# Moving chunk totals through memory in a hybrid trunk kernel, and reordering two small steps

## What is computed

```python
log_a = log_sigmoid(ab @ w_alpha + b_alpha) / B_GATE_TAU          # (S, 256), TAU = 16
g = cumsum(log_a over the 64 tokens of a chunk)
g_end = g[last token of the chunk]                                # the chunk's total
k_dec = k * exp(g_end - g)                                        # decay from token to chunk end
dS = k_dec^T v                                                    # per chunk and head
S_c = exp(g_end) * S_{c-1} + dS                                   # 8 chunks
o_t = q_t S_c
```

## Time and profile before

| | |
|---|---|
| median of 3 runs | 926.05 us (925.83 to 926.31) |
| the profiled execution | 926.16 us |
| its span, first to last instruction | 924.4 us |
| TensorE busy | 916.8 us |
| DVE busy | 609.8 us |
| ACT busy | 390.1 us |
| mean granted TensorE clock | 0.999 |

### The profile page before, as it was taken

One profiled execution on the slowest core, in us unless ns is written; L12 is line 12 of the kernel. 1 busy time (PEld: TensorE's weight loads), 2 busy tenths in 40 slices (PEclk: granted clock), 3 DMA queues, 4 the chain that ended last, 5 costly groups with the idle time before them and its releaser, 6 DMA issues.

```text
span 924.4 us, 13093 instructions
## 1 busy us (share of the span) xinstructions
PE 916.8 (99%) x5092; PEld 752.6 (81%) x5092; DVE 609.8 (66%) x1006; ACT 390.1 (42%) x728; POOL 31.7 (3%) x68
## 2 busy tenths in 40 slices
PE   9999999999999999999999999999999999999997
PEld 7988888888888777888889888888888887778886
DVE  7976468448567877575459655674567668876834
ACT  7453335224543454432444433442363425553324
POOL 0000000000000001000000000000000000100000
PEclk9999999999999999999999999999999999999999
DMA  8424325232534345422233423253235333444542
GB/s 294 126 93 137 114 69 159 91 102 83 154 113 134 90 137 161 137 90 92 92 115 94 125 92 112 62 169 96 88 114 160 103 115 115 133 143 137 150 124 91
DMA packets 42909, 110.98 MB, mean 120 GB/s; under 512 B 8608, under 2 KB 11552, under 8 KB 42720
## 3 DMA queue, kind: packets, MB, share of 16 engines
q1 hardware_dynamic: 36736, 100.62, 34.2%
q10 hardware_dynamic: 4064, 5.33, 2.1%
q0 software_dynamic: 2048, 4.20, 1.6%
HBM read 85.41 MB, written 2.23 MB: 95 GB/s over the span
## 4 chain that ended last, share of the span: by engine, by line
PE 94%; DVE 2%; ACT 2%; DMA 1%; SPq 1%; issue 0%; DVEq 0%; ACTq 0%
PE ring L671 72%; PE nat L671 9%; PE nat L879 3%; PE aux L902 2%; PE nat L858 1%; PE nat L686 1%; PE nat L685 1%; PE nat L687 1%; DMA raw<-pieces 1%; PE ring L686 1%; PE ring L685 1%; PE ring L687 1%; PE nat L749 1%; DVE merged L1227 1%; DVE w_lo L1249 1%; ACT work L1146 1%
## 5 line engine op out<-in xcount | busy, mean ns | idle before, releaser
L671 PE MATMUL ring<-act_hi,w_hi 128*128 128x512 f32 x784 | 307.9, 393 | 0.0
L671 PE MATMUL ring<-act_lo,w_hi 128*128 128x512 f32 x784 | 305.4, 390 | 0.0
L671 PE MATMUL ring<-act_hi,w_lo 128*128 128x512 f32 x784 | 305.1, 389 | 0.0
L919 ACT ACTIVATE w_hi<-raw 128x1024 fp32r<-128x1024 f32 x152 | 161.7, 1064 | 334.2 <-PE ring L671 260.5
L1249 DVE TENSOR_TENSOR w_lo<-raw,w_hi 128x1024 fp32r<-128x1024 f32 x152 | 184.6, 1216 | 97.8 <-ACT w_hi L919 97.6
L671 PEld LDWEIGHTS ring<-act_hi,w_hi 128*128 128x128 f32 x784 | 147.1, 188 | 38.0 <-issue 8.1
L671 PEld LDWEIGHTS ring<-act_hi,w_lo 128*128 128x128 f32 x784 | 147.2, 188 | 31.0
L671 PEld LDWEIGHTS ring<-act_lo,w_hi 128*128 128x128 f32 x784 | 147.2, 188 | 29.7
L1600 DVE SCALAR_TENSOR_TENSOR gates<-ring,rstd 128x512 f32<-128x512 f32 x72 | 49.3, 685 | 78.4 <-PE ring L671 78.3
L671 PE MATMUL ring<-y_hi,w_hi 128*128 128x512 f32 x192 | 74.9, 390 | 0.0
L671 PE MATMUL ring<-y_hi,w_lo 128*128 128x512 f32 x192 | 74.7, 389 | 0.0
(11 more groups left out here) (237 smaller groups left out, 1037.7 us busy)
## 6 DMA issues: line engine op xcount, KB each, us to landing
raw<-pieces SPq DMA_DIRECT2D x152, 512.0 KB, 3.5
bank_g<-work SPq DMA_DIRECT2D x80, 64.0 KB, 2.7
lat<-work SPq DMA_DIRECT2D x48, 64.0 KB, 2.8
bank_g<-work POOLq DMA_DIRECT2D x40, 64.0 KB, 2.5
bank_g<-work ACTq DMA_DIRECT2D x40, 64.0 KB, 3.2
xt<-x_t SPq DMA_DIRECT2D x8, 256.0 KB, 5.2
bank_a<-work SPq DMA_DIRECT2D x32, 64.0 KB, 2.0
bank_g<-bank_a SPq DMA_DIRECT2D x16, 128.0 KB, 3.9
```

The lines of the kernel that those rows point to most:

```text
L671: mm = pe.matmul(dst, stationary, moving, start=start and i == 0, stop=stop and i == 2)
L919: nc.scalar.activation(w_hi[:, n % HL, :], raw[:, n % RAW, :], ACT.Copy).then_inc(hi_split.sem, 1)
```

## The change

1. The chunk totals. The last column of each chunk in `later`, which was zero, now holds 1/TAU for the whole chunk, so the product of `gla_decay` has the chunk's total in the row of its last token. ACT takes Exp twice: once for all rows into `ends` (which lies where `soft` was), once with a per-partition factor `keep` (0 for the last token of a chunk, else 1) into `dec`. In `gla_end` 0, ACT saves the two total rows of each token tile to memory; in `gla_end` 1 it waits for these two saves, and issues two loads that read them back with channels on the partitions, straight into `decay`. The TensorE work of L812 and L815, the copy and the small Exps are gone, and `gla_end` no longer uses the `aux` bank. `gla_state` waits for the loads.
2. The tanh of the last gate piece of branch A moves from before `PUKV` to behind it. `y_lo` 3 stays where it was.
3. In branch C, `gate_c` 0 moves ahead of `divide_c` 2, and `y_hi`, `y_lo` of that output each move by one place.

```diff
@@ make_schedule
-        (63, ("y_hi", 3)),
-        (64, ("y_lo", 3))))
+        (63, ("y_hi", 3))))
     last_gate = todo.pop()
     piece(PUKV)
-    todo.append(last_gate)
+    step(last_gate, ("y_lo", 3))
...
-        (24, ("divide_c", 2)),
-        (25, ("gate_c", 0), ("turn_c", 2)),
-        (26, ("y_hi", TT)),
-        (27, ("y_lo", TT), ("send", 4)),
+        (24, ("gate_c", 0), ("divide_c", 2)),
+        (25, ("y_hi", TT), ("turn_c", 2)),
+        (26, ("y_lo", TT)),
+        (27, ("send", 4)),
...
-AUX = [s for s in SCHEDULE if s[0] in ("rms", "rstd_nat", "gla_end", "latent")]
+AUX = [s for s in SCHEDULE if s[0] in ("rms", "rstd_nat", "latent")]
@@ TensorE
-                    elif name == "gla_end":
-
-                        aux_bank(layer, u)
-                        if i == 0:
-                            for t in range(TT):
-                                mm = pe.matmul(aux[32 * t:32 * t + 32, 0:256], member, log_a[:, t, :], start=True, stop=True)
-                        else:
-                            for j in range(2):
-                                mm = pe.transpose(aux[:, j * P:(j + 1) * P], totals[:, j * P:(j + 1) * P], ident)
@@ ACT
-                        nc.scalar.activation(dec, nat_gate, ACT.Exp).then_inc(dec_set.sem, 1)
+                        nc.scalar.activation(ends, nat_gate, ACT.Exp).then_inc(ends_set.sem, 1)
+                        nc.scalar.activation(dec, nat_gate, ACT.Exp, scale=keep).then_inc(dec_set.sem, 1)
                     elif name == "gla_end":
-                        act.wait_ge(aux_ready.sem, aux_ready.at(layer, u + 1))
                         if i == 0:
-                            nc.scalar.activation(totals, aux[:, 0:256], ACT.Copy).then_inc(aux_free.sem, 1)
+                            act.wait_ge(ends_set.sem, ends_set.at(layer, 1))
+                            for c in range(2):
+                                act.dma_start(ends_dram[:, c:c + 1, :].rearrange("t c n -> c t n"), ends[CHUNK * c + CHUNK - 1:CHUNK * c + CHUNK, :, :]).then_inc(ends_saved.sem, 16)
                         else:
+                            act.wait_ge(ends_saved.sem, ends_saved.at(layer, 32))
                             for j in range(2):
-                                one = nc.scalar.activation(decay[:, NC * j:NC * j + NC].rearrange("p (t c) -> p t c", t=TT),
-                                                           aux[:, j * P:(j + 1) * P].rearrange("p (t m) -> p t m", t=TT)[:, :, 0:2],
-                                                           ACT.Exp)
-                            one.then_inc(aux_free.sem, 1)
+                                act.dma_start(decay[:, NC * j:NC * j + NC],
+                                              ends_dram[:, :, j * P:(j + 1) * P].rearrange("t c p -> p (t c)"), allow_slow_non_contiguous=True).then_inc(ends_placed.sem, 16)
@@ DVE
-                        dve.wait_ge(aux_free.sem, aux_free.at(layer, AUX.index(("gla_end", 1)) + 1))
+                        dve.wait_ge(ends_placed.sem, ends_placed.at(layer, 32))
@@ constants
+    for c in range(2):
+        out[t // CHUNK == c, LATER + CHUNK * c + CHUNK - 1] = 1 / B_TAU
-    out[:, MEMBER:MEMBER + 2] = (t[:, None] // CHUNK == np.arange(2)[None, :]) / B_TAU
+    out[:, KEEP] = t % CHUNK != CHUNK - 1
```

More of the change, by code:

```diff
@@ L289 @@
 PARAMS = 20
-IDENT, MEMBER = 0, 128
+IDENT, KEEP = 0, 128
 K_TABLE = 130
@@ L306, in at, with build_hybrid_trunk @@
         return layer * self.per_layer + (self.before + max(n, 1 - self.before))
-def build_hybrid_trunk(nc, x_t, pieces, params, alpha, tables, consts, final_g, out, k_rope_dram):
+def build_hybrid_trunk(nc, x_t, pieces, params, alpha, tables, consts, final_g, out, k_rope_dram, ends_dram):
     with ExitStack() as ctx:
@@ L352, in build_hybrid_trunk @@
         alpha_raw = bank_a[:, 2048 + P:2048 + P + DEPTH * 256].rearrange("p (l n) -> p l n", l=DEPTH)
-        later, member = bank_a[:, 2048:2048 + P], con[:, MEMBER:MEMBER + 32]
+        later, keep = bank_a[:, 2048:2048 + P], con[:, KEEP:KEEP + 1]
         prob = [*(work[:, i, :] for i in range(3)), bank_a[:, 3072:3584]]
@@ L381, in build_hybrid_trunk @@
         warm = merged[:, 7, :]
-        totals = work[:, 6, 0:256]
         o_nat = prob
@@ L395, in build_hybrid_trunk @@
         soft = gates[:, 8:10, :].rearrange("p a (t n) -> p (a t) n", t=2)
+        ends = soft
         log_a = gates[:, 10:12, :].rearrange("p a (t n) -> p (a t) n", t=2)
@@ L456, in build_hybrid_trunk @@
         gate_in, gate_log, decay_in, dec_set = sig("gate_in", 1), sig("gate_log", 1), sig("decay_in", 1), sig("dec_set", 1)
+        ends_set, ends_saved, ends_placed = sig("ends_set", 1), sig("ends_saved", 32), sig("ends_placed", 32)
         k_dec_set, v_a_set, v_b_set = sig("k_dec_set", TT), sig("v_a_set", TT), sig("v_b_set", TT)
@@ L1827 @@
     k_rope_dram = nc.dram_tensor("k_rope_dram", (C_ROPE, S), F32, kind="Internal").ap()
-    build_hybrid_trunk(nc, *aps, out, k_rope_dram)
+    ends_dram = nc.dram_tensor("ends_dram", (TT, 2, B_HEADS * B_DK), F32, kind="Internal").ap()
+    build_hybrid_trunk(nc, *aps, out, k_rope_dram, ends_dram)
     r = run_bass_kernel_spmd(nc, [arrays], core_ids=[0])
```

## The result

| | before | after |
|---|---|---|
| median of the runs | 926.03 us (925.6 to 926.33, 18 runs) | 928.13 us (926.44 to 928.84, 18 runs) |
| ratio | | 1.0018, 95% interval 1.0011 to 1.0025 |
| profiled execution, its span | 926.16, 924.4 us | 926.77, 925.0 us |

The account below looks back on a forecast made before the run. TensorE, busy 916.8 of 924.4 us, was taken as the bound. Waits +3.2, less 2 x 0.3 and 2 x 0.12 for moved steps, gave +2.3 us on 926.05: 928.3 us, with an 8-in-10 range of 924.8 to 934.8.

Parts of the forecast that it names:

- TensorE's bound: Whole kernel: TensorE is busy 916.8 of 924.4 us, so only removed matmuls or new TensorE waits move the time.
- the wait before the second latent product: TensorE would newly wait there for DVE's release of the aux bank, about 2.6 us in each layer.
- The saved matmuls: TensorE work of the chunk totals: removing four matmuls (0.77 us) and two transposes (0.22) saves 1.0 us per layer.
- The chain on ACT: ACT's queue from `ends` set to the rough root: 7.18 us, delaying TensorE 1.7 and 1.5 us, sum +3.2.
- Saves issued and landed: ACT's saves of the totals: 0.60 us to issue the first, 2.4 from issue to landing of the second.
- The two loads: ACT's issues of the two loads that read the totals back, queued after the saves land: 2.0 us.
- The three copies: Three DMAs that ACT issues before the rough root: 2.13 us, bounds 1.5 and 2.6.
- The load issue: ACT issuing one load of 1,024 single floats: taken as 1.0 us, bounds 0.33 and 2.6.
- one by one: Rival on ACT's loads: issue grows with single elements, 2.6 us a load, +8.7 us, 934.8 us; chance 0.23.
- cheap loads: Rival on ACT's loads: an issue costs 0.33 us like any weight load, -0.4 us, 925.7 us; chance 0.30.
- The moved steps: Tanh behind the latent expansion gains 0.3 us per layer; latent output gated ahead of the divisions gains 0.12 per layer.
- The other side: Rival: ACT's queue is short enough that TensorE keeps the whole gain, 2.8 us, giving 923.2 us; chance 0.12.

Follow-up runs that it names:

- E3: The changed kernel with the wait for the saves and the two loads moved behind the first latent product: 923.04 us median, ratio 0.9968.
- E2: The kernel before with only the tanh and the latent output's gate moved, totals as before: 925.27 us median, ratio 0.9991.
- E4: The changed kernel with each load reading 128 rows of 8 neighbouring floats instead of 1,024 single floats, so totals are misplaced: 926.02 us median, ratio 1.0.
- E5: The changed kernel run again, nothing altered: 926.47 to 926.99 us (6 runs), 927.77 (1), 928.31 to 928.6 (4).
- E7: The changed kernel with the wait for the saves and the loads behind the rough root in layer 1 only: 925.14 to 925.55 us (7 runs), 926.7 to 926.99 (4).
- E8: The changed kernel with both loads of layer 0 issued a second time, into a tile that nothing reads: 929.44 to 930.71 us, 5 runs.
- E1: The changed kernel with the moved tanh and latent-output gate taken back, totals still through memory: 927.62 us median, ratio 1.0023.
- E6: The changed kernel with the wait for the saves and the loads behind the rough root in layer 0 only: 924.23 to 924.75 us, 11 runs.

## Why the prediction came out as it did

- **TensorE's bound, and the wait before the second latent product.** Right, and shown: the wait is there, on the step named, in both layers, and E3 removes it with one moved step. Its size was not: about 2.6 us in each layer was forecast, 1.83 and 1.19 came. The saved matmuls are worth 1.0 us per layer, as worked out: E3 is 2.2 us faster than E2, which has the same moved steps; 0.2 of it is the hold that layer 1 already had in the earlier trace rows.
- **The chain on ACT.** The mechanism was right, its terms were too long. Forecast 7.18 us from `ends` set to the rough root, measured 71.72 - 65.12 = 6.6 in layer 0 and 527.25 - 521.30 = 5.95 in layer 1. Saves issued and landed: 3.0 forecast, 3.18 and 2.55 measured. The 3.0 hides two errors: the first save's issue took 1.22 us in layer 0 and about 0.7 in layer 1, not 0.60, and from the second save's issue to the landing it was 1.9 in both, not 2.4. (The 2.0 that the prediction takes from the Trainium skill, "DMA: Bandwidth & Descriptors", Anatomy of one DMA, is given there for transfers that GpSimd issues; for these saves, which ACT issues, the profile shows the 1.9.) The two loads: 2.0 forecast, 1.5 measured, an issue being 0.64 us in the median and not 1.0. The three copies: 2.13 forecast, 1.9 measured; SP's eight issues ended at 70.60, when ACT had begun the second of the three, which may be why; no run tests it. So the holds cost +1.4 us over before, not +3.2. This is the term that was mis-sized.
- **The load issue.** Taken from a row of copies between partitions that came behind another issue, 1.08; it was nearer to the plain loads' 0.33. One packet per float is true (E4), but the issue did not grow in proportion; the rival "one by one" is refuted, "cheap loads" was closer (0.42 for rows, 0.64 for single floats, against its 0.33).
- **The moved steps.** Forecast 0.84 us, measured 0.7. The tenth that DVE's copies could take back was taken back.
- **The clock.** Not in the forecast at all. It costs 1.7 us in 11 of the 18 executions of the changed kernel, and in 4 or 5 of E5's 11. That the forecast 928.3 fell on the median 928.13 is luck, because two errors cancelled: a chain 1.8 us too long, and 1.7 us of slower clock that was not counted. Without the clock the time is 926.6, a difference that by the prediction's own limit of 1.85 us cannot be told from no change, which had a chance of 0.37. The median moves with the share of the upper group: 928.13 in 18 runs, 926.99 in the 11 of E5.
- **The other side,** the whole gain at 923.2, is what E3 measures: 923.04. It takes a different place in the queue, not lower bounds in all terms.

## What to carry to other kernels

A wait for a DMA in an in-order queue costs whatever stands behind it: before putting a save and a reload there, ask what the queue owes next, and put that first. Here the same transfers cost 3.6 us or nothing, by one step's place, and removing work from the bounding engine gained only once its next condition had been moved too. Where times fall into two clusters, compare the clusters before trusting a median, and look in a profile of each for the stretch where the clock differs; the mean over the whole execution is too coarse.

## What the runs showed of the hardware

Behind a TensorE wait of 1.8 us between dense matmuls, E7's profile shows about 3.4 us at a granted clock of 0.50, and so does E8's behind one of 3.3 us; the profiles of the changed kernel and of E5 show none behind the same 1.8. By their times, the upper groups cost 1.6 to 1.8 us more and hold 11 of 18 executions (changed kernel), 4 of 11 (E1), 4 of 11 (E7) and 4 or 5 of 11 (E5); with waits of up to 1.2 us (E6) or 1.4 us (E4) it is 0 of 11 each, with 3.3 us 5 of 5 (E8). What decides between executions with the same 1.8 us wait stays open. A DMA that gathers 1,024 single floats took 0.64 us to issue and 3.3 us to land, against 0.42 and 1.7 for the same bytes in 128 rows.
